# A hybrid attention and FFN layer on one core: another order of loads and of work in the first stage, other banks for the key products, late sums in halves

## The reference, cut to what matters

```python
mod_x = jnp.split((jax.nn.silu(c) @ w_ada[l] + b_ada[l])[:, None, :], 6, axis=-1)
mod_c = jnp.split((jax.nn.silu(c_ctx) @ w_ada[l] + b_ada[l])[None, None, :], 6, axis=-1)
...
hc = modulate(xc, norm_g[l, 0], mod_c[0], mod_c[1])      # 256 context tokens
h = modulate(x, norm_g[l, 0], mod_x[0], mod_x[1])        # 1024 tokens, width 1024
qa, ka, va, u, qw, kw, vw, gate = split_mixer_inputs(h @ w_in[l])   # hc likewise
qa, ka, qw, kw = (apply_rope(...) for each)
```

## Time and profile before

| what | value |
| --- | --- |
| median of 3 runs | 1960.22 us (1957.39 to 1963.56) |
| profiled execution | 1961.0 us, of which its span 1959.2 us |
| PE busy | 1816.6 us, 93% of the span |
| DVE / ACT / POOL busy | 57% / 39% / 43% |
| mean granted clock of PE | 0.967 of full |
| first stage, from the trace | its last matmul starts at 572.46 us; the next stage's first at 582.17 us |

### The profile page before, as it was taken

One profiled execution on the slowest core, in us unless ns is written; L12 is line 12 of the kernel. 1 busy time (PEld: TensorE's weight loads), 2 busy tenths in 40 slices (PEclk: granted clock), 3 DMA queues, 4 the chain that ended last, 5 costly groups with the idle time before them and its releaser, 6 DMA issues. The chain is left out here.

```text
span 1959.2 us, 26541 instructions
## 1 busy us (share of the span) xinstructions
PE 1816.6 (93%) x9312; PEld 1535.5 (78%) x9312; DVE 1110.1 (57%) x1559; ACT 760.9 (39%) x1433; POOL 836.1 (43%) x516
## 2 busy tenths in 40 slices
PE   6897999999979999697999989789999999899998
PEld 4896888887767888597988878668888888688886
DVE  2436578878848888375753346484544445322322
ACT  2434333334326777354530025543333333232332
POOL 0124668766515967400001212375555555243433
PEclk9898999999989999798989999899999999899999
DMA  7233333435566665203013342212222121354552
GB/s 273 85 98 116 126 111 135 166 129 213 196 173 166 143 154 135 92 2 77 0 66 123 148 148 89 84 54 97 76 85 95 66 96 64 121 191 145 199 176 91
DMA packets 84204, 235.25 MB, mean 120 GB/s; under 512 B 11025, under 2 KB 24721, under 8 KB 83986
## 3 DMA queue, kind: packets, MB, share of 16 engines
q1 hardware_dynamic: 84114, 234.09, 36.5%
HBM read 180.19 MB, written 53.87 MB: 119 GB/s over the span
## 5 line engine op out<-in xcount | busy, mean ns | idle before, releaser
L677 POOL TENSOR_TENSOR ring<-raw_w,ring 128x512 fp32r<-128x512 f32 x120 | 181.1, 1523 | 162.8 <-ACT ring L566 162.8
L78 PE MATMUL psum<-h_hi,ring 128*128 128x512 f32 x400 | 156.3, 391 | 8.4 <-ACT z L612 4.2
L80 PE MATMUL psum<-h_hi,ring 128*128 128x512 f32 x400 | 155.7, 389 | 0.0
L79 PE MATMUL psum<-h_lo,ring 128*128 128x512 f32 x400 | 155.6, 389 | 0.0
L2466 DVE TENSOR_TENSOR u_lo<-stage,u_hi 128x1024 fp32r<-128x1024 f32 x44 | 58.2, 1325 | 159.7 <-ACT u_hi L2426 159.7
L78 PE MATMUL psum<-u_hi,uf_hi 128*128 128x512 f32 x352 | 137.7, 391 | 9.7 <-POOL uf_lo L2449 9.4
L2449 POOL TENSOR_TENSOR uf_lo<-u_f,uf_hi 128x512 fp32r<-128x512 f32 x44 | 79.9, 1817 | 156.0 <-ACT uf_hi L2428 155.8
L79 PE MATMUL psum<-u_lo,uf_hi 128*128 128x512 f32 x352 | 137.4, 390 | 0.0
L80 PE MATMUL psum<-u_hi,uf_lo 128*128 128x512 f32 x352 | 137.4, 390 | 0.0
L566 ACT ACTIVATE ring<-raw_w 128x512 fp32r<-128x512 f32 x120 | 73.7, 627 | 136.1 <-DVE raw_w L802 58.5
L78 PE MATMUL psum<-i_m_hi,i_hi 128*128 128x512 f32 x264 | 103.9, 393 | 4.8 <-DVE i_m_lo L2175 4.8
(11 more groups left out here) (323 smaller groups left out, 5105.0 us busy)
## 6 DMA issues: line engine op xcount, KB each, us to landing
stage<-in_w_ffn_out SPq DMA_DIRECT2D x44, 512.0 KB, 3.6
raw_w<-in_w_pairs SPq DMA_DIRECT2D x40, 512.0 KB, 4.6
qk_dram<-room SPq DMA_DIRECT2D x26, 512.0 KB, 3.6
room<-in_w_ada SPq DMA_DIRECT2D x24, 512.0 KB, 5.4
gates_dram<-ost SPq DMA_DIRECT2D x24, 512.0 KB, 3.0
b_g<-gates_dram SPq DMA_DIRECT2D x8, 1536.0 KB, 7.9
stage<-in_w_ff SPq DMA_DIRECT2D x22, 512.0 KB, 4.6
i_raw<-in_w_ff SPq DMA_DIRECT2D x22, 512.0 KB, 4.4
```

What stands on the lines that cost most here:

```text
L78: pe.matmul(out, sh, mh, start=first, stop=False, skip_group_check=onto)
L79: pe.matmul(out, sh, ml, start=False, stop=False, skip_group_check=onto)
L80: return pe.matmul(out, sl, mh, start=False, stop=last, skip_group_check=onto)
L677: pool.tensor_tensor(w_lo[i], source(p, i), w_hi[i].bitcast(F32), ALU.subtract).then_inc(w_lo_ready, 1)
```

## The change

It moves work within the first stage and changes the order of waits; every product, sum and transfer is still made once.

- SP loads `cond` first, then pieces of `w_ada`; after the second come the small tensors, and after every second one of the first eight a token tile of its own (`x0_in`).
- PE does the first six channel blocks' pieces, then `transposes(0)`, then puts the transposes of units 1 to 4 before pieces 12 to 15, and those of 5 to 7 at the end. ACT cuts the value weights between `modulate(3)` and after; DVE does the same with the low parts between its units. `statistics(1)` follows directly, and `statistics(2)` comes before the units 8 to 15.
- `SPREAD` puts the transposes of units 8 to 11 in tile 2 and of 12 to 15 in tile 3.
- The window key's products use banks 5 and 6 and wait for one context result fewer. The first three key stores come ahead of SP's wait for the sums and of the cosine and sine loads, and ACT and DVE take the context results earlier in their lists.
- The sigmoid of a pair's last quarter comes after the next pair's `first_product`.
- The late sums are made two by two: two pieces behind `rope_swap`, ahead of `read_early`, and two behind `rope_sum`, ahead of `shared`. SP refills two buffers at a time within the pair.

```diff
@@ -200 +200 @@
         small_in, x_in = sem("in_small"), [sem(f"in_x{c}") for c in range(3)]
+        cond_in = sem("in_cond")
+        x0_in = [sem(f"in_x0_{t}") for t in range(4)]
...
@@ -227 +229 @@
-        SPREAD = {2: {6: 8, 7: 9}, 3: {0: 10, 1: 11, 3: 12, 4: 13, 5: 14, 6: 15},
+        SPREAD = {2: {0: 8, 2: 9, 4: 10, 6: 11}, 3: {0: 12, 2: 13, 4: 14, 6: 15},
...
@@ -256 +258 @@
         def _(sp):
-            for dst, src in ((cond[:], io["cT"]), (ada_b[:], io["b_adaT"]), (norm_g[:], io["norm_gT"]), (ident[:], io["ident"]),
-                             (sub_g[:], io["sub_g"])):
-                sp.dma_start(dst, src).then_inc(small_in, 16)
-            sp.dma_start(spare[:, 0:4 * HD], io["da_lambda"].to_broadcast([P, 4 * HD])).then_inc(small_in, 16)
+            sp.dma_start(cond[:], io["cT"]).then_inc(cond_in, 16)
...
             cv = io["ctx"].rearrange("(t p) d -> p t d", p=P)
-            sp.dma_start(xt[0][:], xv[:, 0:4, :]).then_inc(x_in[0], 16)
...
                 sp.dma_start(ada[i % ADA_BUFS], io["w_ada"][i // 2 + KC * (i % 2)]).then_inc(ada_in[i % ADA_BUFS], 16)
+                if i == 1:
+                    for dst, src in ((ident[:], io["ident"]), (ada_b[:], io["b_adaT"]), (norm_g[:], io["norm_gT"]),
+                                     (sub_g[:], io["sub_g"])):
+                        sp.dma_start(dst, src).then_inc(small_in, 16)
+                    sp.dma_start(spare[:, 0:4 * HD], io["da_lambda"].to_broadcast([P, 4 * HD])).then_inc(small_in, 16)
+                if i in (1, 3, 5, 7):
+                    t = i // 2
+                    sp.dma_start(xt[0][:, t, :], xv[:, t, :]).then_inc(x0_in[t], 16)
...
@@ -306 +312 @@
             store_v(9)
-            sp.wait_ge(t2_sum, 1)
-            sp.wait_ge(t3_sum, 1)
-            sp.dma_start(cos, io["cos"]).then_inc(table_in, 16)
-            sp.dma_start(sin, io["sin"]).then_inc(table_in, 16)
             for j in range(5):
+                if j == 3:
+                    sp.wait_ge(t2_sum, 1)
+                    sp.wait_ge(t3_sum, 1)
+                    sp.dma_start(cos, io["cos"]).then_inc(table_in, 16)
+                    sp.dma_start(sin, io["sin"]).then_inc(table_in, 16)
...
@@ -322 +329 @@
+            def load_late(first, count):
+                for n in range(first, first + count):
+                    sp.dma_start(late_w[n % 4], io["w_ada"][3 * KC + n]).then_inc(late_in[n % 4], 16)
+
...
                     load_raw(p + 2)
+                if p == LATE[0]:
+                    sp.wait_ge(rx_ready, 1 + 2 * len(order["r"]))
+                    load_late(0, 4)
...
                 if p in LATE:
-                    first = 4 * LATE.index(p)
-                    if first:
-                        sp.wait_ge(late_used, first)
-                    else:
-                        sp.wait_ge(rx_ready, 1 + 2 * len(order["r"]))
-                    for j in range(4):
-                        sp.dma_start(late_w[j], io["w_ada"][3 * KC + first + j]).then_inc(late_in[j], 16)
+                    done = 4 * LATE.index(p)
+                    for n in (done + 2, done + 4):
+                        sp.wait_ge(late_used, n)
+                        if n + 2 < 2 * KC:
+                            load_late(n + 2, 2)
+                if p == LATE[-1]:
+                    sp.dma_start(io["late"], late_acc).then_inc(late_out, 16)
                 if p == LATE[-1] + 1:
-                    sp.wait_ge(late_used, 2 * KC)
-                    sp.dma_start(io["late"], late_acc).then_inc(late_out, 16)
...
@@ -378 +390 @@
+            BETWEEN = {12: 1, 13: 2, 14: 3, 15: 4}
...
             for k in range(KC):
+                if k == 1:
+                    pe.wait_ge(small_in, 80)
...
                 for i in (2 * k, 2 * k + 1):
+                    if i in BETWEEN:
+                        transposes(BETWEEN[i])
...
@@ -390 +407 @@
                     turn_rows(k - 1)
-                transposes(k)
+                if k == 5:
+                    transposes(0)
+            transposes(5)
             turn_rows(KC - 1)
+            transposes(6)
+            transposes(7)
...
@@ -424 +445 @@
             for n in (1, 0):
-                pe.wait_ge(kc_lo, 4 - n)
+                pe.wait_ge(kc_lo, 3 - n)
...
                 for k in range(KC):
-                    mm = parts_product(pe, banks[7 - n], (kw_hi[4][:, k, :], kw_lo[4][:, k, :]),
+                    mm = parts_product(pe, banks[6 - n], (kw_hi[4][:, k, :], kw_lo[4][:, k, :]),
...
@@ -463 +484 @@
                 a, b = CH[c][0], CH[c][-1] + 1
-                act.wait_ge(x_in[c], 16)
+                if c:
+                    act.wait_ge(x_in[c], 16)
                 for t in CH[c]:
+                    if c == 0:
+                        act.wait_ge(x0_in[t], 16)
...
@@ -513 +537 @@
                 act.wait_ge(cut_lo["T4"], KH)
-                act.activation(xr[0][:, n * HALF:(n + 1) * HALF], banks[7 - n], ACT.Copy).then_inc(kq_copied, 1)
-
-            act.wait_ge(small_in, 96)
+                act.activation(xr[0][:, n * HALF:(n + 1) * HALF], banks[6 - n], ACT.Copy).then_inc(kq_copied, 1)
+
+            act.wait_ge(cond_in, 16)
...
             act.activation(lamd[:, 2:4], lamd[:, 0:2], ACT.Exp).then_inc(lam_exp, 1)
-            statistics(0)
-            for u in range(0, 8):
-                modulate(u)
-            for k in range(KC):
+            def v_weight_hi(k):
...
                 act.activation(v_hi[:, k, :], v_raw[:, k, :], ACT.Copy).then_inc(vh_ready, 1)
+
+            statistics(0)
+            for u in range(0, 3):
+                modulate(u)
+            for u in range(3, 8):
+                v_weight_hi(u - 3)
+                modulate(u)
+            for k in range(5, KC):
+                v_weight_hi(k)
+            statistics(1)
             values(0)
+            statistics(2)
             values(1)
-            statistics(1)
...
                 modulate(u)
-            statistics(2)
...
@@ -572 +602 @@
                 moving_hi("T1", T1, T1f, k)
+            k_context(2)
             weight_hi(0, 0)
-            k_context(2)
+            k_context(3)
+            k_context(4)
             weight_hi(0, 1)
-            k_context(3)
...
                 moving_hi("T3", T3, T3f, k)
-            k_context(4)
...
@@ -634 +664 @@
                 first_product(p)
+                if p:
+                    gate(p - 1, c21, 2)
...
@@ -652 +684 @@
                     weight_hi(p + 1, 5)
-                gate(p, c12, 1)
...
                     weight_hi(p + 1, 6)
-                gate(p, c21, 2)
+                gate(p, c12, 1)
+            gate(NP - 1, c21, 2)
...
@@ -758 +790 @@
-            v.wait_ge(small_in, 96)
...
             ch.did(v.tensor_tensor(keep["silu_x"][:], cond[:, 0, :], econd[:, 0, :], ALU.mult))
+            v.wait_ge(small_in, 80)
...
@@ -774 +806 @@
             ch.link(v.tensor_scalar(sub_g[:], sub_g[:], 1.0 - LAM_INIT, None, ALU.mult))
-            statistics(0)
-            copy_rows(0)
-            for k in range(KC):
-                if k + 1 < KC:
-                    copy_rows(k + 1)
-                modulation(k)
-                unit(k)
-            for k in range(KC):
+            def v_weight_lo(k):
...
                 v.tensor_tensor(v_lo[:, k, :], v_raw[:, k, :], v_hi[:, k, :].bitcast(F32), ALU.subtract).then_inc(vl_ready, 1)
+
+            copy_rows(0)
+            for k in range(3):
+                copy_rows(k + 1)
+                modulation(k)
+            statistics(0)
+            copy_rows(4)
+            modulation(3)
+            copy_rows(5)
+            modulation(4)
+            unit(0)
+            unit(1)
+            copy_rows(6)
+            modulation(5)
+            unit(2)
+            v_weight_lo(0)
+            unit(3)
+            v_weight_lo(1)
+            copy_rows(7)
+            modulation(6)
+            unit(4)
+            v_weight_lo(2)
+            unit(5)
+            modulation(7)
+            v_weight_lo(3)
+            for k in (6, 7):
+                unit(k)
+                v_weight_lo(k - 2)
+            v_weight_lo(6)
+            v_weight_lo(7)
             statistics(1)
+            statistics(2)
...
                 unit(u)
-            statistics(2)
...
@@ -820 +875 @@
                 moving_lo(v, "T1", T1, T1f, k)
+            k_context(2)
...
             v.tensor_tensor(T1f, B22f, T1f, ALU.subtract).then_inc(t2_sum, 1)
+            k_context(3)
+            k_context(4)
             v.wait_ge(t2_sum, 1)
+            s13(0)
             v.tensor_tensor(T4f, T4f, T1f, ALU.subtract).then_inc(t4_sum, 1)
-            k_context(2)
-            s13(0)
-            k_context(3)
             s2(0)
-            k_context(4)
...
@@ -897 +952 @@
-            def late_sums(first):
-
+            def late_sums(p, j):
+
+                if p not in LATE:
+                    return
                 silu_x = keep["silu_x"]
-                if first == 0:
+                n = 4 * LATE.index(p) + j
```

(25 more changed lines are left out.)

15 lines of the change are left out of this document (removed).

## The result

The changed kernel takes **1931.53 us** (median of 4 runs, 1929.13 to 1932.21) beside 1960.43 (1957.39 to 1963.56) for the kernel before: 28.9 us less, a ratio of 0.985 (95% interval 0.9833 to 0.9868). The forecast was 1924.7, the range 1912 to 1937. The time lies in the range, 6.8 us above the forecast. The profiled execution took 1931.34 us, its span 1929.2.

A forecast was written before the change was run, and what follows sets the result against it. PE, busy 93% of the span, bounds the kernel; only its idle and slow time can be won. 15 + 5 + 10 + 1.5 + 4 = 35.5 us off 1961.0 gives 1925.5, median 0.8 lower: 1924.7, range 1912 to 1937.

The forecast's parts named there:

- A: Start to the end of value tile 0: earlier first piece and reordered work save 15 us (11 to 17).
- rival (3): DVE/POOL lock: four collisions of 1.26 us, and as much before pair 0, 3 us each: 1931; chance 0.14.
- B: Value tiles 1 to 9: two token waits and slow clock go, 0.8 us lost at tile 3; saves 5 us (3 to 6).
- C: Key products and pair 0: 12.5 us won, 2.9 us lost at product 3; saves 10 us (6 to 12.5).
- D: Pair loop: waits of 4.1 and 4.2 us go, 6.8 us lost from pair 14; saves 1.5 us (-1 to 8.3).
- E: End of the stage: head loads begin about 10 us earlier, last store sooner; saves 4 us (0 to 4.5).
- (1): Pair 14: first two late pieces come in time or the wait is covered; pair loop saves 8.3 us, 1917.9; chance 0.12.
- (2): Conditioning: early pieces come late because DMA engines share time among everything queued; A halves, 1932 us; chance 0.17.
- (4): Value tiles: waits for `v_lo` in tile 0 keep the clock low for ten tiles, costing 59 us: 1984; chance 0.02.
- (5): A and B only shift idle time to the key products; end unmoved, within 0.3%; chance 0.01.

The follow-up runs named there:

- e2: Kernel before with only the key products' banks, waits, stores and list orders changed: 1956.49 us, ratio 0.9963.
- e10: The changed kernel run again, unaltered: 1930.04 us, ratio 0.984.
- e4: Changed kernel with the first half of the late sums behind `read_early` in all four pairs: 1927.84 us, ratio 0.9815.
- e5: As e4, but in pair 14 the first half of the sums behind `s2`, the second behind `lower_left`: 1924.58 us, ratio 0.9813.
- e8: Changed kernel with both moved sigmoids, of the last and the second quarter, put back: 1930.78 us in one execution, 0.983 of the kernel before.
- e3: Changed kernel with the late sums, on DVE and on SP, as before the change: 1928.95 us, ratio 0.9817.
- e11: As e5, plus ACT's `second_product` and window key copies directly behind `first_product` in pair 0, and pair 14's late pieces issued ahead of raw weights: 1920.70 us, ratio 0.9786.
- e12: Changed kernel with the four token tiles issued ahead of the pieces of `w_ada`: 1935.6 us in one execution.
- e7: Changed kernel with both value weight parts made behind all eight token units, on ACT and DVE: 1934.54 us, ratio 0.9857.
- e1: Kernel before with only the changes up to the last value tile (loads, conditioning, token units, value weights): 1942.93 us, ratio 0.9895.
- e6: Changed kernel with the window key's products in banks 6 and 7 as before, waiting for one context result more: 1935.49 us in one execution.

## Why the prediction was right or wrong

**A** was right to 0.7 us. The first piece landed at 4.97 us (forecast near 5.0), `silu` was there, and the DMA wait of 14.0 us in the earlier trace rows is now one of 5.1 and one of 1.24 us. Value tile 0 was reached at 44.34 (forecast 43.7) and ended near 53.8 (53.2). The 1.24 us were not in the forecast, which had the pieces ahead of PE from 20 us on. The collisions are as priced; timelines of POOL and DVE, after:

```profile
45.18 1.29 POOL L697 TENSOR_TENSOR h_lo<-room,h_hi 128x512 fp32r<-128x512 f32 x1 [3.27 <-DVE h_hi L780]
45.33 1.83 DVE L811 TENSOR_TENSOR v_lo<-v_raw,v_hi 128x640 fp32r<-128x640 f32 x1
...
49.20 3.39 DVE L811 TENSOR_TENSOR v_lo<-v_raw,v_hi 128x640 fp32r<-128x640 f32 x3
```

and the group of all eight (ns, smallest, median, largest; first and last start):

```profile
L811 DVE TENSOR_TENSOR v_lo<-v_raw,v_hi x8: 812/819/1918, 38.9 to 51.8; 128x640 fp32r<-128x640 f32 x8
```

One took 1.83 us, and of the three in 3.39 us one took 1.92: two collisions, 2.1 us in all, not the four of rival (3). The Trainium skill (SBUF — State Buffer, "SBUF: two separate sides") says that of a GpSimd operation and such a DVE one, whichever starts first blocks the other until it is through. The rows agree: DVE's started 0.15 us behind POOL's and took 1.83 us beside a median of 0.82.

**B** was right: no token wait is left, and the new one at tile 3 is 0.73 us at 71.39 (forecast 0.8). The 0.8 us above the forecast is inside its bound; part of it is a wait of 0.56 us for ACT's copies (L493) in the value tiles, which the forecast did not count and which is gone too.

**C**: the front is right to 0.1 us (12.6 of 12.5), and so is the statement that something else would be late in pair 0. Its size was nearly right (2.8 us of waits and 0.8 of slow restarts, for 2.9) and its place half right: the forecast had all of it at product 3, for L636. There it was 0.61 us, 0.18 us stood ahead of it, and 2.01 us came at product 5, for L642. I had walked ACT's list to the first copy only and took the second for granted, though the same list, with a cut that waits for DVE, lies between them. What the step left out is that a wait of 2.0 us may bring a clock drop (e2, e10).

**D** failed: -1.2 instead of 1.5. The gains came as forecast, and slightly more: the four waits of 1.03 us are gone and are worth 4.9 us: the lead rises by 1.28 at each of the first three, and by 1.03 at the fourth. The three waits of 4.2 us for L612 (now L642) are gone, and two of 0.37 and 0.86 us for DVE's `z` (L897) are new in pairs 16 and 17; with what is around them this gave 3.6. The loss in pair 14 was forecast at 5.5 and 1.3 us, 6.8 together, and measured 9.7 (lead 34.1 to 24.4). Its mechanism is the one of the forecast, as e4 and e5 show. Two terms of it were mis-sized:

- *The wait*, 6.73 instead of 5.5. The transfers and the sums were right: `z` was there at 441.44 + 0.68 = 442.12, 13.0 us after SP issued the raw weights (forecast 473.8 - 460.94 = 12.9). What was wrong is PE's due time against that issue. The forecast has that the sigmoid itself "costs nothing later, the store has a pair's time". But the raw weights and the late pieces stand behind that store in SP's list. With the sigmoids moved, two operations of DVE in pair 13 fell beside POOL operations and took 1.20 us longer (e8), and the store with all that is behind it came 1.2 us later against PE (2.0 in place of 0.8 us). It is the kind of collision that rival (3) priced for other places; the forecast did not look for it here. Which of the two moved sigmoids does how much was not tried. In e8, where PE's wait is kept, the forecast's sum gives 5.5 - 1.03 = 4.5, and 4.55 was measured.
- *The clock behind it*, which the forecast had at nothing. Windows of the changed kernel (length, busy us and count of PE, PEld, DVE, ACT and POOL, PEclk, DMA, GB/s):

```profile
440.00:443.00 3.00, 0.74 (x2) 0.67 (x3) 3.00 (x8) 0.00 (x0) 0.00 (x0) 0.50 0.00 0
443.00:447.00 4.00, 4.00 (x11) 3.13 (x10) 4.00 (x15) 0.63 (x1) 2.41 (x1) 0.50 0.76 262
447.00:451.00 4.00, 4.00 (x17) 3.18 (x16) 3.96 (x9) 1.34 (x3) 2.10 (x2) 0.88 1.02 369
451.00:455.00 4.00, 4.00 (x19) 3.32 (x18) 3.97 (x4) 2.90 (x6) 4.00 (x3) 1.00 0.93 373
```

PE had stood since 435.5, and the granted clock fell at 437.7, while it stood. Between 443 and 447 us it issued 11 matmuls, where 4 / 0.228 = 17 fit at the full clock. The lead is 27.2 us at the first matmul behind the wait (442.26) and 24.4 at 448.7, from where it holds: 2.8 us for the slow clock. I had this price in hand, from the value tiles, and in this part counted none. The wait of 1.3 us in pair 15, on the other side, did not come.

**E** was right: a gap of 4.72 us where 9.32 stood, 4.6 (forecast 4). e3 shows that it belongs to the earlier late sums: with the old ones the gap is 8.51.

**The rest, 2.9 us, stays open.** Of it 0.3 us lie outside the span (2.1 us around it instead of 1.8). From the next stage's first matmul to the end of the span the kernel before needed 582.17 to 1959.2, 1377.0 us, and the changed one 549.59 to 1929.2, 1379.6. This code is the same in all the kernels here, and in their fourteen profiles it took between 1375.7 (e11) and 1380.5 us (e4), e10 1379.1. So the difference of 2.6 us is within what these stages vary by from one execution to the next, and the profile of before has a short one. Where the lead changes there, PE's half-clock periods lie differently, but their sum after the first stage (some 102 us before, 101 after) does not explain it. A sum that is made against one profiled execution carries an uncertainty of some 3 us for that reason alone, and mine had no term for it.

**The rivals.** (1) fell by the pair 14 wait. (2) fell by the start at 5.11 us and by e12. (3) is wrong in number, not in kind: two collisions in A, and two more in pair 13 that nobody had counted. The cuts ahead of pair 0 were no slower than before (median 1778 ns in both). (4) did not show: the clock stayed at full through the ten tiles, in spite of the waits of 0.66 and 0.69 us in tile 0, but in e7 one wait of 3.25 us there came with 6.8 us at half. (5) fell by e1.

## What to carry to other kernels

PE's idle time adds up where PE is the bound: in four of the five parts the gain came out within 1 us of its forecast. For that one has to walk each other engine's list on to the next thing PE needs, through every copy and not only the first. When a wait of PE disappears, the other engines don't all get earlier by the same amount. DVE and POOL operations can then meet, or overlap for longer, and every transfer that stands behind their results in one issuing queue gets later against PE. Before moving work ahead of a result that PE needs, look whether that work waits for a transfer: here one DVE stall of 7.9 us, with the slow clock behind it, ate the 8.5 us that the moved sigmoids and the halved sums had won in the pair loop. Placing the work later, where the transfers had nearly landed, gave some 5 us back; placing it just behind the result (e4) only moved the wait.

## What the runs showed of the hardware

- A wait of 1.03 us cost 1.28 us of lead at three places of four: the matmuls behind it start slower. (The first takes 0.47 us in place of 0.39.) At the fourth the changed kernel had a short pause of its own, of 0.15 us.
- Behind a wait of 2.0 us, the granted clock was at 0.50 for 3.4 us in six of ten profiles with that wait in pair 0 (e2, e3, e4, e6, e7, e10), and not in four (the first of the changed kernel, e5, e8, e12), with the same work in the pair around it. Between the two profiles of the changed kernel this was 1.2 us.
- Behind a wait of 6.7 us it was at half for 10.2 us in one profile of the changed kernel (from 437.7, while PE still stood) and for 6.8 in the other (e10, 6.84 us, from 441.9), behind 5.92 us in e4 for 6.8, behind 4.55 us in e8 for 3.4, and behind 3.25 us in e7 for 6.8.
- Transfers of 512 KB that follow each other at the head of the span land 1.27 to 1.32 us apart, in the order of issue: four more ahead of the first piece made it 5.1 us later (e12).
- A DVE operation on two inputs of 128x1024 (`rope_sin`, `rope_sum`) ended 1.08 to 1.09 us after the POOL operation that was running when it began, in three cases (changed kernel 408.71 and 425.73, e8 412.89), and so took 1.72 to 2.86 us.
- PE's first matmuls start 0.21 us apart and, 5 to 6 us later, 0.11 us (15 and 30 in windows of 3 us, from 5.2 and from 11.2 us in the changed kernel; 15 in 3 us and 10 in 1 us, from 14.1 and from 19.0, in the kernel before). The profile prints a granted clock of 1.00 for both, so at the start of a span its PEclk can't be taken as it stands.
